# A second attention taken out of its loop: every step of every head at a fixed step of the weight ring, across the borders of the units

## What is computed

```python
h = rms_norm(x, ln_gain[l]); proj = h @ w_in[l]
q, k, v, z_att, u, z_ssm, g_att, g_ssm = jnp.split(proj, splits, axis=-1)
q = rms_norm(q.reshape(bsz, seq, 8, 2, 64), q_norm_gain[l])      # the same for k
s = jnp.einsum('bqhcd,bkhcd->bhcqk', q_blk, k) * scale           # causal mask, softmax
w = p[:, :, 0] - lam * p[:, :, 1]                                # two softmaxes of each head
attn = rms_norm(jnp.einsum('bhqk,bkhe->bqhe', w, v), subln_gain[l]) * (1.0 - lam_init)
y_att = attn.reshape(bsz, seq, D_ATT) * jax.nn.silu(z_att)       # y_ssm: state space branch and GLU
merged = sigmoid(g_att) * (y_att @ w_proj_att[l]) + sigmoid(g_ssm) * (y_ssm @ w_proj_ssm[l])
x = x + merged @ w_out[l]
```

## Time and profile before

| what | value |
|---|---|
| median of 3 runs | 2401.95 us (2401.73 to 2402.02) |
| profiled execution, its own time | 2403.9 us |
| its span in the trace | 2402.2 us |
| mean granted TensorE clock | 0.982 of full speed |
| PE busy | 2269.6 us, 94% |
| DVE / ACT / POOL busy | 1463.5 / 1192.6 / 457.7 us (61 / 50 / 19%) |
| moved by DMA | 426.41 MB, mean 178 GB/s |
| GLU's last matmul starts | 1984.68 us |
| pairs A | about 1991.9 to 2173.5 us |
| pairs B | about 2173.5 to 2309 us |

### The profile page before, as it was taken

One profiled execution on the slowest core, in us unless ns is written; L12 is line 12 of the kernel. 1 busy time (PEld: TensorE's weight loads), 2 busy tenths in 40 slices (PEclk: granted clock), 3 DMA queues, 4 the chain that ended last, 5 costly groups with the idle time before them and its releaser, 6 DMA issues.

```text
span 2402.2 us, 33351 instructions
## 1 busy us (share of the span) xinstructions
PE 2269.6 (94%) x11622; PEld 1902.4 (79%) x11622; DVE 1463.5 (61%) x1634; ACT 1192.6 (50%) x1804; POOL 457.7 (19%) x460
## 2 busy tenths in 40 slices
PE   4999999999999979999999999989999898989999
PEld 3888988788888768888888888869866686767887
DVE  3656669644554565555555555565998966665554
ACT  5455556644444445555555555554444444453443
POOL 2011385000000101211221121110656620100000
PEclk9999999999999989999999999999999999999999
DMA  6544444566666836666666666655555544445665
GB/s 184 176 149 144 145 123 150 172 189 193 190 188 195 261 117 198 200 207 198 198 206 196 200 206 196 199 172 176 171 171 172 179 149 141 147 133 169 183 193 165
DMA packets 214167, 426.41 MB, mean 178 GB/s; under 512 B 13984, under 2 KB 14272, under 8 KB 213312
## 3 DMA queue, kind: packets, MB, share of 16 engines
q1 hardware_dynamic: 206336, 398.64, 54.2%
q0 software_dynamic: 7744, 26.62, 3.4%
HBM read 414.71 MB, written 10.49 MB: 177 GB/s over the span
## 4 chain that ended last, share of the span: by engine, by line
PE 73%; DVE 11%; issue 8%; POOL 3%; ACT 3%; DMA 1%; SPq 0%; DVEq 0%; ACTq 0%; POOLq 0%
PE acc L1730 20%; PE acc L1732 20%; PE acc L1731 20%; DVE w_lo L1079 3%; PE acc L1722 3%; PE acc L1724 3%; PE acc L1725 3%; PE tps L1745 1%; POOL slab_f_f L567 1%; ACT w_hi L639 1%; DMA raw<-in_w_out_dram 1%; DVE k_t L1531 1%; POOL slab_f_f L568 1%; PE sides L1785 1%; PE tps L1803 1%
## 5 line engine op out<-in xcount | busy, mean ns | idle before, releaser
L1079 DVE TENSOR_TENSOR w_lo<-raw,w_hi 128x1024 fp32r<-128x1024 f32 x752 | 967.2, 1293 | 780.1 <-ACT w_hi L639 775.3
L639 ACT ACTIVATE w_hi<-raw 128x1024 fp32r<-128x1024 f32 x752 | 793.0, 1059 | 933.9 <-PE acc L1732 768.9
L1730 PE MATMUL acc<-w_hi,h_hi 128*128 128x512 f32 x1440 | 578.9, 402 | 20.5 <-DVE w_lo L1079 8.3
L1731 PE MATMUL acc<-w_lo,h_hi 128*128 128x512 f32 x1440 | 566.8, 394 | 0.0
L1732 PE MATMUL acc<-w_hi,h_lo 128*128 128x512 f32 x1440 | 566.4, 393 | 0.0
L1730 PEld LDWEIGHTS acc<-w_hi,h_hi 128*128 128x128 f32 x1440 | 274.5, 191 | 92.9 <-issue 23.7
L1732 PEld LDWEIGHTS acc<-w_hi,h_lo 128*128 128x128 f32 x1440 | 274.1, 190 | 59.1
L1731 PEld LDWEIGHTS acc<-w_lo,h_hi 128*128 128x128 f32 x1440 | 274.9, 191 | 54.1
L1730 PE MATMUL acc<-w_hi,slab_dg_r 128*128 128x512 f32 x768 | 300.2, 391 | 3.2 <-DVE w_lo L1079 3.2
L1732 PE MATMUL acc<-w_hi,slab_dg_r 128*128 128x512 f32 x768 | 299.5, 390 | 0.0
L1731 PE MATMUL acc<-w_lo,slab_dg_r 128*128 128x512 f32 x768 | 299.4, 390 | 0.0
(11 more groups left out here) (374 smaller groups left out, 2439.5 us busy)
## 6 DMA issues: line engine op xcount, KB each, us to landing
raw<-in_w_in_dram SPq DMA_DIRECT2D x328, 512.0 KB, 3.8
raw<-in_w_mlp_up_dram SPq DMA_DIRECT2D x128, 512.0 KB, 3.7
raw<-in_w_mlp_down_dram SPq DMA_DIRECT2D x128, 512.0 KB, 4.6
raw<-in_w_out_dram SPq DMA_DIRECT2D x64, 512.0 KB, 4.6
raw<-in_w_rnn_proj_dram SPq DMA_DIRECT2D x32, 512.0 KB, 3.9
raw<-in_w_attn_proj_dram SPq DMA_DIRECT2D x32, 512.0 KB, 4.6
trig_scratch<-tmp POOLq DMA_DIRECT2D x32, 256.0 KB, 4.0
raw<-in_w_proj_ssm_dram SPq DMA_DIRECT2D x16, 512.0 KB, 5.5
```

What stands on the lines that cost most here:

```text
L639: nc.scalar.activation(w_hi[:, j % RING], raw[:, j % RING], ACT.Copy).then_inc(hi_ready, 1)
L1079: V.tensor_tensor(w_lo[:, j % RING], raw[:, j % RING], w_hi[:, j % RING].bitcast(F32), ALU.subtract)\
L1730: T.matmul(o, hi[:, k, c], wh, start=first, stop=False)
L1731: T.matmul(o, hi[:, k, c], wl, start=False, stop=False)
```

## The change

The loop is written out, and the steps of a head are placed by a table. Ring steps are counted from the start of the first pair A, 12 to a pair; head n begins at `SOFT2_AT[n]` = 2, 8, 14, 20, ... (every 6 steps), and `beside_a` turns a global place into a unit and its slot, the first unit of B included. For a head that begins at `at`: PE `scores2` at, `turn_w` at + 4, `by_v2` at + 5; ACT `exps2` at + 2, `w_copy` at + 4, `o_squares` at + 5; DVE `soft2` at, `combine` at + 3, mean square at + 5, `gate` at + 6. An odd head so ends in the next pair, the eighth in B's first unit.

The norm of q and k of the next pair is made half a pair early: square on ACT (at 3 of a pair, before on DVE), sums on DVE (4), power on GpSimd, multiplies on DVE (7), turn on PE (end of 9), copy on ACT (10). That of the first pair moves into the GLU units; its turn is at step 0, its copy at 1. The turn of a pair's gated output comes at the end of step 15, its high and low parts at 16, in the next pair. `combine` no longer scales the first softmax (the division by its sum goes into the RMS norm behind it: `o_squares` is scaled, GpSimd multiplies once more); `o_out` and the copy to `stg` are gone, `gate` reads PSUM. GpSimd writes the mask before the GLU units. PE's wait for `glu_lo` moves behind the first unit of the first pair. The scores' eight matmuls take turns between the two halves of the rows. Semaphores and `T_B`, `H_B` follow. Bodies that only change their indices are left out below.

```diff
+SOFT2_AT = [12 * (n // 2) + 2 + 6 * (n % 2) for n in range(8)]
+def beside_a(places):
+    tables_ = [{} for _ in range(9)]
+    for at, hook in places:
+        i, s = divmod(at, 12)
+        n, start = (8, 48) if i == 4 else (2 * i + (s >= 8), 12 * i + 8 * (s >= 8))
+        tables_[n].setdefault(at - start, []).append(hook)
+    return tables_
...
-    pool.wait_ge(glu_ready, 2)
+    def root_qk(i):
+        pool.wait_ge(qk_ms, i + 1)
+        pool.tensor_tensor(qk_rstd_, qk_ms_, neg_half[:, 0:16], ALU.pow).then_inc(qk_rstd, 1)
+    def root_o(n):
+        of = att2_of[n % 2]
+        pool.wait_ge(o_ms, n + 1)
+        chain.link(pool.tensor_tensor(of[:, 14:16], of[:, 14:16], neg_half[:, 0:2], ALU.pow))
+        pool.tensor_tensor(of[:, 14:16], of[:, 14:16], of[:, 0:2], ALU.mult).then_inc(o_rstd, 1)
+    pool.wait_ge(y5_ready, 8)
...
-    with pool.Fori(0, NH) as i:
-        pool.wait_ge(qk_ms, i + 1)
-        pool.tensor_tensor(att2[:, 16:32], att2[:, 0:16], neg_half[:, 0:16], ALU.pow).then_inc(qk_rstd, 1)
-        pool.wait_ge(o_ms, i + 1)
-        pool.tensor_tensor(att2[:, 60:64], att2[:, 56:60], neg_half[:, 0:4], ALU.pow).then_inc(o_rstd, 1)
+    root_qk(0)
+    for i in range(NH):
+        if i < NH - 1:
+            root_qk(i + 1)
+        root_o(2 * i)
+        root_o(2 * i + 1)
...
+    def qk_square(i):
+        qk = dg_tok.rearrange("p t (w c) -> p t w c", c=1024)[:, :, 0:2, i * SEQ:(i + 1) * SEQ]
+        if i:
+            act.wait_ge(qk_ms, i)
+        nc.scalar.activation(qk_squares[i], qk, ACT.Square).then_inc(qk_squared, 1)
     for c in range(2):
-        steps(None, 0, G_GLU + c * 4, subgroups=4)
+        steps(None, 0, G_GLU + c * 4, {0: [lambda: qk_square(0)]} if c == 0 else None, subgroups=4)
...
-    with act.Fori(0, NH) as i:
...
+    places = [(1, lambda: qk_copy(0))]
+    for i in range(NH):
+        places += [(12 * i + 16, lambda i=i: y2_high(i)), (12 * i + 5, lambda i=i: z_tanh(i))]
+        if i < NH - 1:
+            places += [(12 * i + 3, lambda i=i: qk_square(i + 1)), (12 * i + 10, lambda i=i: qk_copy(i + 1))]
+    for n, at in enumerate(SOFT2_AT):
+        places += [(at + 2, lambda n=n: exps2(n)), (at + 4, lambda n=n: w_copy(n)), (at + 5, lambda n=n: o_squares(n))]
+    beside = beside_a(places)
+    for i in range(NH):
+        steps(None, 0, G_A + PAIR * i, beside[2 * i])
+        act.wait_ge(pe_used, G_A + PAIR * i + S)
         act.wait_ge(acc_free[(U_A - 1) % 2], i + ((U_A - 1) // 2 + 1))
         for t in range(TT):
             ins = nc.scalar.activation(tmp[:, t, :], tok(acc[U_A % 2])[:, t, :], ACT.Tanh, scale=half_rstd[:, t:t + 1])
         ins.then_inc(acc_free[U_A % 2], 1)
+        steps(None, 0, G_A + PAIR * i + S, beside[2 * i + 1], 4)
...
+    gate_unit(None, 0, beside[8])
...
-        steps(None, 0, G_GLU + c * 4, subgroups=4)
+        steps(None, 0, G_GLU + c * 4, {1: [lambda: qk_mean_square(0)]} if c == 0 else {1: [lambda: qk_norm(0)]}, subgroups=4)
...
+    def combine(n):
+        of = att2_of[n % 2]
+        dve.wait_ge(exp2_ready, n + 1)
+        chain.link(V.reciprocal(of[:, 0:4], of[:, 8:12]))
+        chain.link(V.scalar_tensor_tensor(of[:, 2:4], of[:, 8:10], lam4[:, 6:7], of[:, 2:4], ALU.mult, ALU.mult))
+        for t in range(TT):
+            at = slice(0, P) if t == 0 else slice(P, 3 * P)
+            ins = V.scalar_tensor_tensor(probs2[0][:, at], probs2[1][:, at], of[:, 2 + t:3 + t], probs2[0][:, at],
+                                         ALU.mult, ALU.add)
+            if t == 0:
+                chain.mark(ins)
+        ins.then_inc(w2_ready, 1)
...
+    def gate(n):
+        h, of = n % 2, att2_of[n % 2]
+        dve.wait_ge(o_rstd, n + 1)
+        chain.wait()
+        for t in range(TT):
+            z_ = keep[:, t, h * P:(h + 1) * P]
+            ins = V.scalar_tensor_tensor(z_, tps[:, (4 + t) * P:(5 + t) * P], of[:, 14 + t:15 + t], z_, ALU.mult, ALU.mult)
+            if t == 0:
+                chain.mark(ins)
+        ins.then_inc(gated, 1)
...
+    places = []
+    for i in range(NH):
+        places += [(12 * i + 16, lambda i=i: y2_low(i)), (12 * i + 6, lambda i=i: z_gain(i))]
+        if i < NH - 1:
+            places += [(12 * i + 4, lambda i=i: qk_mean_square(i + 1)), (12 * i + 7, lambda i=i: qk_norm(i + 1))]
+    for n, at in enumerate(SOFT2_AT):
+        places += [(at + 5, lambda n=n: o_mean_square(n)), (at + 6, lambda n=n: gate(n)),
+                   (at, lambda n=n: soft2(n)), (at + 3, lambda n=n: combine(n))]
...
+    def turn_qk(i):
+        pe.wait_ge(qk_staged, i + 1)
+        if i:
+            pe.wait_ge(gated, 2 * i - 1)
+        if i >= 2:
+            pe.wait_ge(y2_out, i - 1)
+        for t in range(TT):
+            for b in range(QPC):
+                ins = T.transpose(tps[:, b * SEQ + t * P:b * SEQ + (t + 1) * P], stg[:, t, b * P:(b + 1) * P], ident[:, :])
+        ins.then_inc(qk_turned, 1)
...
+    def turn_w(n):
+        pe.wait_ge(w2_ready, n + 1)
+        if n:
+            pe.wait_ge(w2_copied, n)
+        if n % 2 == 0 and n:
+            pe.wait_ge(y2_out, n // 2)
+        if n % 2 and n < 7:
+            pe.wait_ge(qk_copied, n // 2 + 2)
+        for b in range(3):
+            ins = T.transpose(tps[:, b * P:(b + 1) * P], probs2[0][:, b * P:(b + 1) * P], ident[:, :])
+        ins.then_inc(w2_turned, 1)
...
+    def turn_y(i):
+        pe.wait_ge(gated, 2 * i + 2)
+        for t in range(TT):
+            for b in range(2):
+                ins = T.transpose(tps[:, b * SEQ + t * P:b * SEQ + (t + 1) * P], keep[:, t, b * P:(b + 1) * P], ident[:, :])
+        ins.then_inc(y2_turned, 1)
...
+    places = [(0, 0, lambda: turn_qk(0))]
+    for i in range(NH):
+        places.append((12 * i + 15, 1, lambda i=i: turn_y(i)))
+        if i < NH - 1:
+            places.append((12 * i + 9, 1, lambda i=i: turn_qk(i + 1)))
+    for n, at in enumerate(SOFT2_AT):
+        places += [(at, 0, lambda n=n: scores2(n)), (at + 4, 0, lambda n=n: turn_w(n)), (at + 5, 0, lambda n=n: by_v2(n))]
+    beside = []
+    for tables_ in zip(*(beside_a([(at, f) for at, e_, f in places if e_ == e]) for e in range(2))):
+        beside.append({2 * s + e: hooks for e in range(2) for s, hooks in tables_[e].items()})
+    for i in range(NH):
+        unit(None, 0, G_A + PAIR * i, 0, U_A + 2 * i, h_hi, h_lo, hooks=beside[2 * i])
+        if i == 0:
+            pe.wait_ge(glu_lo, 2)
+        unit(None, 0, G_A + PAIR * i + S, 0, U_A + 2 * i + 1, slab_fr[:, 8:16, :], slab_hr[:, 8:16, :], k_tiles=K8,
+             hooks=beside[2 * i + 1])
     pe.wait_ge(tps_free, T_B)
+    unit(None, 0, G_B, 0, U_B, h_hi, h_lo, hooks=beside[8])
```

More of the change, by code:

```diff
@@ new lines, in soft2 @@
+            def soft2(n):
+                of = att2_of[n % 2]
+                dve.wait_ge(s2_ready, n + 1)
+                if n == 0:
+                    dve.wait_ge(mask2_ready, 1)
+                else:
+                    dve.wait_ge(w2_turned, n)
+                for c in range(2):
+                    ins = V.scalar_tensor_tensor(probs2[c], side[c][:, 0:3 * P], 0.125, mask[:, :], ALU.mult, ALU.add)
+                    if c == 0:
+                        chain.mark(ins)
+                ins.then_inc(s2_read, 1)
+                dve.wait_ge(s2_read, n + 1)
+                chain.wait()
+                for c in range(2):
+                    chain.mark(V.tensor_reduce(of[:, 2 * c:2 * c + 1], probs2[c][:, 0:P], AX.X, ALU.max))
+                    chain.mark(V.tensor_reduce(of[:, 2 * c + 1:2 * c + 2], probs2[c][:, P:], AX.X, ALU.max))
+                chain.wait()
+                V.tensor_scalar(of[:, 4:8], of[:, 0:4], -1.0, None, ALU.mult).then_inc(neg2_ready, 1)
@@ L1678, in merged_low @@
                                        ALU.mult, ALU.subtract).then_inc(tps_free, 1)
-            steps(None, 0, G_B)
+            steps(None, 0, G_B, beside[8])
             with dve.Fori(0, NH - 1) as i:
@@ L1956, in scores2 @@
+            def scores2(n):
+                h = n % 2
+                if h == 0:
+                    pe.wait_ge(qk_copied, n // 2 + 1)
+                if n:
+                    pe.wait_ge(s2_read, n)
+                for t in range(TT):
                     for c in range(2):
                         at = slice(64 * c, 64 * c + 64)
-                        for t in range(TT):
-                            ins = T.matmul(side[c][:, t * P:t * P + (t + 1) * P], qk_c[at, h, t * P:(t + 1) * P],
-                                           qk_c[at, 2 + h, 0:(t + 1) * P], start=True, stop=True)
@@ L1980, in _ @@
-                unit(i, PAIR, G_A, 2, U_A, h_hi, h_lo,
-                     hooks={5: [lambda: turn(i, 2, T_A)], 7: [lambda: scores2(0)], 12: [lambda: turn_w(0)],
-                            13: [lambda: scores2(1)], 14: [lambda: by_v2(0)]})
-                unit(i, PAIR, G_A + S, 2, U_A + 1, slab_fr[:, 8:16, :], slab_hr[:, 8:16, :], k_tiles=K8,
-                     hooks={4: [lambda: turn_w(1)], 5: [lambda: by_v2(1)]})
-                turn(i, 2, T_A + 1, blocks=2)
```

(12 more changed lines are left out.)

243 lines of the change are left out of this document (93 added, 150 removed).

## The result

| what | before | after |
|---|---|---|
| median, us | 2401.98 (2401.73 to 2403.35, 4 runs) | 2369.14 (2367.56 to 2369.82, 4 runs) |
| ratio, 95% interval | | 0.9856 (0.9844 to 0.9868) |
| profiled execution, its time and span, us | 2403.9, 2402.2 | 2369.07, 2367.4 |
| mean granted TensorE clock | 0.982 | 0.986 |
| stretch of the prediction, us | 233.3 | 197.1 |

The kernel is faster by 33 to 35 us; 2367.3 had been forecast, with 2363 to 2377 around it. By the page of the kernel after, against the earlier trace rows, PE has the same 11622 matmuls and 7 us less of (generously counted) busy time in 35 us less of span.

What follows compares the result with a forecast made beforehand. TensorE, busy 94% of the span, was taken as the bound, held up by order. Floor 196.0 plus 2.6 us of waits made 198.6 against 233.3, so 34.7 off the median 2401.95: 2367.3 us, range 2363 to 2377.

Steps and rivals of the forecast that it cites:

- stretch of the prediction: From GLU's last matmul to the matmul behind the first turn of the pairs B: 233.3 us before, 198.6 forecast.
- Floor of 196.0: PE's work in the stretch without waits: 171.7 us of ring work plus 24.3 of small work, against 233.3.
- Two long groups of waits gone: In the pairs, PE's waits for the gated output (10.1 us in four) and `combine` (8.4 in eight) go.
- Even head 0.4 to spare, odd head none: At `turn_w`: even heads' `combine` ends at 7.1 against PE's 7.5 us; odd heads wait 0 to 0.2.
- Rival 2: Each `turn_w` still waits about 1.4 us for its weights, 9.6 us together: 2376.9 us; chance 0.12.
- Late copy of q and k, 1.0: First pair: ACT's copy ends at 1993.5, PE wants the scores at 1992.5: a 1.0 us wait.
- Table load, 1.2: One load remains before the first exponential and delays `turn_w(0)` by 1.2 us; three passes lose theirs.
- Slow matmuls go with the waits: Matmuls at half clock behind idle time, as at the border to pairs B, go with the preceding waits.
- The moved norm and the output's turn at no cost: First norm fits the GLU slots, costing nothing (1.4 us uncovered); output's turn follows the gate by a step, no wait.
- The scores' order at nothing: Alternating row halves in the scores' eight matmuls gains nothing; the other bound was 3.4 us for all.
- The sum: Stretch of 196.0 + 2.6 us of waits = 198.6, less 233.3: 34.7 us gained; median 2367.3.
- Rival 1: DVE's split waits for GpSimd's whole power: 2.4 us in three pairs, 7.2: 2374.5 us; chance 0.10.

Runs made afterwards that it cites:

- The kernel without any wait: Kernel after with a one-column exponential in GLU's third ACT slot and first q and k copy at step 0: 2367.87 us, stretch 195.2.

## Why the prediction was right

Each step against what the runs show:

- **Floor of 196.0.** The kernel without any wait has 195.2. Within it the errors partly cancel. Bare ring steps run at 0.228 a matmul rather than 0.227, about 1 us more over 756. The turn of the output (0.36 and not 0.57 until the next matmul, four times) and `turn_w` (0.25 and not 0.30, eight times) are cheaper, 1.2 us less, and the matmul behind each piece of small work is 0.09 longer rather than 0.10. In the earlier trace rows the two turns stood behind a wait. I priced work by its rows behind a wait and then took the wait away. Scores (0.86) and the product with v (0.58) were as read.
- **Two long groups of waits gone.** Right; the 18.5 us of the earlier trace rows are 0.9.
- **Even head 0.4 to spare, odd head none.** Right to 0.3 us. `combine` ends at 2044.90 + 0.75 = 2045.65, and `turn_w` starts at 2046.02: 0.37. The odd head ahead of it has 0.15 to spare, where a wait of 0 to 0.2 had been forecast. That `turn_w` half a step early waits in every head confirms that this slack is small. Rival 2, weights late as before, falls: one wait, not eight.
- **Late copy of q and k, 1.0.** The wait is 0.6. I had it end at 1993.5 against 1992.5 on PE; taken from GLU's last matmul, it was to end 8.8 us later and ended 8.5 later, at 1994.56.
- **Table load, 1.2.** It is 0.9, at the place named; and of four loads one is left in the stretch, in ACT's timeline:

```profile
1999.96 1.06 ACT L668 ACTIVATE w_hi<-raw 128x1024 fp32r<-128x1024 f32 x1 [0.73 <-PE acc L1791]
2001.04 1.28 ACT L1049 ACT_TABLE_LOAD   x1
2002.34 0.40 ACT L1049 ACTIVATE tmp<-tmp,att 128x128 f32<-128x128 f32 x1
```

  The Trainium skill (ScalarE activation tables: per-element evaluation and per-set limits, section "Table sets in the compiler and the runtime") says that the compiler places these loads block by block. The traces agree: one load at the head of each pass while the loop stands, at 1990.19, 2037.83, 2082.87 and 2127.87, and one in this stretch once it is written out.
- **Slow matmuls go with the waits.** They went: 26 before, none after, 6 when one wait of 6.5 is put back. But a wait doesn't always bring them. Before, they stand behind three places: the 6.99 us, the first of the four waits of 2.5 and the last (which the 1.6 us follow), and not behind the other two of 2.5; three waits of 2.3 put back bring none. Which waits cost the clock was not forecast, and these rows do not settle it.
- **The moved norm and the output's turn at no cost.** Right, but as a pair only. I had costed the output's turn by itself ("the 10.1 us go"). Alone it brings 6.8, since the wait moves to the norm; and with the norm two steps late 7.5 us are lost again. The same holds at the GLU border, where the 7.0 us were held three times.
- **The scores' order at nothing.** Right.
- **The sum.** Forecast 34.7 on the stretch, measured 36.2: waits 1.1 smaller (1.5 for 2.6), floor 0.4 lower. The median came out 1.8 us above the forecast all the same, since I had taken 2 us off for the profiled execution: before's own time in it, 2403.9, is near the median of 51 runs beside the experiments (2403.4), and the three runs shown first were low. That correction was mis-sized. With 2403.4 the forecast would have been 2368.7, nearer to the 2369.14; but part of that nearness is luck, since the stretch gained 1.5 us more than forecast and the time did not show them.
- **Rival 1, the blocked port,** falls on DVE. DVE's timeline of the kernel after, and below it GpSimd's in the same microseconds:

```profile
2043.29 1.23 DVE L1126 TENSOR_TENSOR w_lo<-raw,w_hi 128x1024 fp32r<-128x1024 f32 x1
...
2044.90 0.75 DVE L1669 SCALAR_TENSOR_TENSOR tmp<-tmp,att 128x128 f32<-128x128 f32 x2
```

```profile
2043.32 3.95 POOL L593 TENSOR_TENSOR att<-att,neg_half 128x16 f32<-128x16 f32 x1 [10.28 <-DVE att L1614]
```

  Split and `combine` last what they last alone (1.22 and 0.75). The power grows from 2.90 to 3.95 us, here and in the next pair. My 0.5 us for the split, carried over from the earlier trace rows, did not come, and nobody waits for the power. I had misread those rows: the GpSimd operation shown there starts 0.64 us behind the split, and another one, at 1925.90, was ahead of it. The timelines hold both orders. Of the kernel before, first the operation that began ahead of the split of the earlier trace rows, then a split that began first, and the GpSimd operations behind it:

```profile
1925.90 0.91 POOL L561 TENSOR_TENSOR tmp<-tmp 128x256 f32<-128x256 f32 x1
...
1930.87 1.22 DVE L1079 TENSOR_TENSOR w_lo<-raw,w_hi 128x1024 fp32r<-128x1024 f32 x1
...
1931.04 1.65 POOL L567 TENSOR_TENSOR slab_f_f<-tmp 128x256 f32<-128x256 f32 x1 [2.54 <-DVE tmp L1535]
...
1932.65 0.73 POOL L568 TENSOR_TENSOR slab_f_f<-tmp 128x256 f32<-128x256 f32 x1
```

  Of the kernel after, the first power, beside the GLU units:

```profile
1970.09 2.93 POOL L593 TENSOR_TENSOR att<-att,neg_half 128x16 f32<-128x16 f32 x1 [23.79 <-DVE att L1614]
...
1970.21 1.23 DVE L1126 TENSOR_TENSOR w_lo<-raw,w_hi 128x1024 fp32r<-128x1024 f32 x1 [0.20 <-ACT w_hi L668]
```

  In the state space stage the one that starts second takes longer: a GpSimd operation of 256 columns takes 1.65 us when it starts 0.17 behind a split and 0.73 with none beside it, and the split then keeps its 1.22; a split that starts 0.24 behind such an operation takes 1.76. The power at 2043.32 starts 0.03 behind its split and is 1.05 longer. The power at 1970.09 starts 0.12 ahead of one, and neither is longer by more than 0.03. The Trainium skill (SBUF — State Buffer, section "Who interferes with whom") lets a VectorE instruction with two SBUF inputs contend with a GpSimd one that reads SBUF, over ports that it calls an exclusive lock, and says that the order of issue decides who blocks. The traces agree on the order. A block for the whole of the first instruction, rival 1, they do not show: the split at 1970.21 would then have waited 2.8 us for the power. No run moves the two against each other.

## What to carry to other kernels

A wait on the bounding engine is often only the first of several: put the operands' whole chains side by side, and ask which one is next late once the wait is gone. Here three stood at one border and two at each pass, and parts of the change that are worth 1 to 7 us alone are worth 36 together. Where every operation has a fixed step in the bounding engine's order, write down for each engine when its slot ends; a table in tenths of us gave the slack within 0.3 us, and half a step on the wrong side of it costs a wait in every head.

Price small work from rows that do not stand behind a wait, and take the reference time from as many runs as there are, not the first three.

## What was not expected of the hardware

- Of a DVE split that reads two SBUF operands and a GpSimd operation beside it, the one that starts second can take longer: GpSimd's power of 16 columns takes 3.95 us in place of 2.90 when it starts 0.03 behind the split, and 2.93 when it starts 0.12 ahead, with the split at 1.23 both times. In the state space stage a split grew to 1.76 behind a GpSimd operation of 256 columns that was 0.24 ahead. This is read from the traces, not tried.
- Idle time and the clock are not additive. With the loop written out, waits fell by 4.1 us and slow matmuls' excess rose by 3.8; in two profiles of one and the same kernel they were 28.2 and 5.6, then 26.0 and 8.4. Nor does each wait bring slow matmuls: the first wait of 2.5 us before does, two of the same length do not, and three of 2.3 and eight of 0.9 to 2.3 us in the variants of after leave the clock at 1.00.
- A first exponential may run 0.02 us behind its table load (2001.04 + 1.28 to 2002.34).
